# A depthwise convolution moved from VectorE to GpSimd, in pieces of 512 columns, with silu and store one chunk later

## What is computed

```python
def causal_dwconv(x, buf, w):
    width = w.shape[0]
    t = x.shape[1]
    xx = jnp.concatenate([buf.astype(x.dtype), x], axis=1)
    y = xx[:, 0:t, :] * w[0]
    for j in range(1, width):
        y = y + xx[:, j:j + t, :] * w[j]
    return y, xx[:, xx.shape[1] - (width - 1):, :]

c, new_buf = causal_dwconv(qkv, conv_buf, conv_w)
c = jax.nn.silu(c)
```

## Time and profile before

| what | value |
|---|---|
| median of 3 runs | 4591.77 us (4585.16 to 4597.04) |
| the profiled execution | 4549.66 us, its span 4548.4 us |
| PE busy | 3964.1 us, 87% |
| DVE busy | 2130.7 us, 47% |
| ACT busy | 1527.5 us, 34% |
| POOL busy | 689.2 us, 15% |
| mean granted TensorE clock | 0.902 of full speed |

### The profile page before, as it was taken

The page is one execution under the profiler, slowest core; times in us unless marked ns, Lnnn a source line. Parts: engine busy times, 40 slices in busy tenths (PEclk is TensorE's granted clock), DMA queues, the critical chain, the costliest instruction groups (busy, mean ns, idle before and its releaser), DMA issues. The chain is left out here.

```text
span 4548.4 us, 51075 instructions
## 1 busy us (share of the span) xinstructions
PE 3964.1 (87%) x19290; PEld 3133.7 (69%) x19290; DVE 2130.7 (47%) x4240; ACT 1527.5 (34%) x2433; POOL 689.2 (15%) x547
## 2 busy tenths in 40 slices
PE   7789787798769876888888769989999999979999
PEld 4445454455358555777777764479999999958777
DVE  5528988998943683333333332224444444430200
ACT  2115555665645233333333321122222222221211
POOL 0100000000000003222222121111111111124443
PEclk9889898999879687778788789999999999989999
DMA  2242222121142102111111013311212121145433
GB/s 92 78 108 64 59 56 69 35 70 36 45 165 73 36 11 69 30 29 33 29 33 31 25 58 107 102 44 37 56 37 56 37 56 37 47 152 168 130 111 112
DMA packets 286836, 298.41 MB, mean 66 GB/s; under 512 B 33599, under 2 KB 231103, under 8 KB 281626
## 3 DMA queue, kind: packets, MB, share of 16 engines
q1 hardware_dynamic: 271278, 256.80, 19.7%
q0 software_dynamic: 2112, 20.97, 1.2%
q10 hardware_dynamic: 13264, 18.25, 1.2%
HBM read 202.15 MB, written 94.10 MB: 65 GB/s over the span
## 5 line engine op out<-in xcount | busy, mean ns | idle before, releaser
L530 PE MATMUL chan_p_g<-ht,chan_w 128*128 128x412 f32 (+1 forms) x1760 | 678.0, 528 | 62.7 <-ACT chan_flat L578 33.7
L914 PE MATMUL up_p_g<-ht_high,up_wh 128*128 128x412 f32 (+1 forms) x1760 | 617.0, 351 | 0.0
L914 PE MATMUL up_p_g<-ht_low,up_wh 128*128 128x412 f32 (+1 forms) x1760 | 615.0, 349 | 0.0
L914 PE MATMUL up_p_g<-ht_high,up_wl 128*128 128x412 f32 (+1 forms) x1760 | 614.8, 349 | 0.0
L530 PEld LDWEIGHTS chan_p_g<-ht,chan_w 128*128 128x128 f32 x1760 | 341.5, 197 | 310.1 <-issue 230.1
L932 ACT ACTIVATE up_pre<-up_p_g 128x412 f32<-128x412 f32 (+1 forms) x220 | 113.3, 515 | 748.0 <-PE up_p_g L914 748.0
L1294 ACT ACTIVATE chan_signed<-chan_sc,chan_trial 128x512 bf16<-128x512 f32 (+6 forms) x224 | 304.9, 1361 | 148.5 <-DVE chan_trial L1349 127.7
L914 PEld LDWEIGHTS up_p_g<-ht_high,up_wh 128*128 128x128 f32 x1760 | 331.3, 188 | 1.6 <-issue 0.4
L914 PEld LDWEIGHTS up_p_g<-ht_low,up_wh 128*128 128x128 f32 x1760 | 331.2, 188 | 1.2
L914 PEld LDWEIGHTS up_p_g<-ht_high,up_wl 128*128 128x128 f32 x1760 | 331.0, 188 | 0.5
L984 DVE TENSOR_SCALAR up_acc<-up_pre,up_taps 128x2048 f32<-128x2048 f32 x44 | 59.3, 1347 | 573.5 <-ACT up_pre L932 573.5
(11 more groups left out here) (549 smaller groups left out, 6874.9 us busy)
## 6 DMA issues: line engine op xcount, KB each, us to landing
down_a<-scratch_act SPq DMA_DIRECT2D x88, 512.0 KB, 3.7
scratch_act<-up_acc SPq DMA_DIRECT2D x22, 1028.0 KB, 5.2
up_w<-in_w_up SPq DMA_DIRECT2D x44, 512.0 KB, 6.4
chan_iq<-scratch_iq SPq DMA_DIRECT2D x28, 512.0 KB, 7.2
scratch_qkv<-chan_acc SPq DMA_DIRECT2D x12, 1028.0 KB, 4.6
mid_raw<-scratch_qkv SPq DMA_DIRECT2D x16, 768.0 KB, 5.3
chan_w<-in_w_in SPq DMA_DIRECT2D x22, 512.0 KB, 4.6
proj_x<-in_x_prompt SPq DMA_DIRECT2D x16, 512.0 KB, 3.5
```

The source lines that it names most:

```text
L530: last = pe.matmul(p_g[u % BANKS][:, 0:cols.stop - cols.start], weights[:, k, :], K.ht[:, k, cols], start=(k == 0), stop=(k == KD - 1))
L914: last = pe.matmul(p_g[u][:, 0:cols.stop - cols.start], wp[s][:, k, :], hp[:, k, cols], start=(k == 0 and m == 0), stop=(k == KD - 1 and m ...
```

## The change

All four taps go to GpSimd, which does them as soon as the five drains of block v are done. [...] Tap 0 is one TENSOR_SCALAR of 2048 columns. The eight sample columns are TENSOR_SCALARs of their own, added with the last piece. Silu and store move one chunk further on: silu after the second group of chunk v + 2, the store after the third.

```diff
+    PART = SEQ // 4
...
+        tmp = c.sb("tmp", [P, PART + DEC])
...
@@ sync
-                    if idx == 3 and n > IQS and kind(n - 1)[0] == "conv":
-                        v = kind(n - 1)[1]
+                    if idx == 2 and n > IQS + 1 and kind(n - 2)[0] == "conv":
+                        v = kind(n - 2)[1]
                         sp.wait_ge(s_silu, v + 1)
                         sp.dma_start(K.d_qkv[v, :, :], acc[v % 2][:, :]).then_inc(s_st[v % 2], 16)
...
@@ scalar
-                    if idx == 3 and n > IQS and kind(n - 1)[0] == "conv":
-                        v = kind(n - 1)[1]
+                    if idx == 1 and n > IQS + 1 and kind(n - 2)[0] == "conv":
+                        v = kind(n - 2)[1]
                         act.wait_ge(s_conv, v + 1)
...
@@ vector
-            dve.wait_ge(s_taps, 64)
-            for n in range(IQS, CHUNKS):
-                for idx in range(NG):
-                    if idx < 4 and n > IQS and kind(n - 1)[0] == "conv":
-                        if idx == 0:
-                            dve.wait_ge(s_evac, n * NG - FROM)
-                        conv(kind(n - 1)[1], idx)
-                    side.until(share(n * NG + idx, KD))
+            for u in range(FROM, CHUNKS * NG):
+                side.until(share(u, KD))
             side.rest()
+
+        @block.gpsimd
+        def _(pool):
+            step = Chain(pool, s_step)
+            pool.wait_ge(s_taps, 64)
+            pool.wait_ge(s_kept, 1)
+            for n in range(IQS, CHUNKS):
+                what, v = kind(n)
+                if what != "conv":
+                    continue
+                src, out = pre[v % 2], acc[v % 2]
+                old = past[:, v, :].rearrange("p (b j) -> p b j", j=3)
+                tap = lambda i: taps[:, i, v:v + 1]
+                last_of = lambda i: old[:, :, i] if i < 3 else src[:, 3 + SEQ:]
+                if v == 0:
+                    pool.wait_ge(s_mm, FROM)
+                if v:
+                    pool.wait_ge(s_conv, v)
+                if v >= 2:
+                    pool.wait_ge(s_st[v % 2], v // 2 * 16)
+                pool.wait_ge(s_evac, (n + 1) * NG - FROM)
+                pool.tensor_scalar(out[:, 0:SEQ], src[:, 0:SEQ], tap(0), None, ALU.mult)
+                pool.tensor_scalar(out[:, SEQ:], last_of(0), tap(0), None, ALU.mult)
+                for i in range(1, 4):
+                    for at in range(0, SEQ, PART):
+                        final = at + PART == SEQ
+                        if final:
+                            pool.tensor_scalar(tmp[:, PART:], last_of(i), tap(i), None, ALU.mult)
+                        step(pool.tensor_scalar(tmp[:, 0:PART], src[:, at + i:at + PART + i], tap(i), None, ALU.mult))
+                        part = out[:, at:] if final else out[:, at:at + PART]
+                        last = pool.tensor_tensor(part, part, tmp[:, :] if final else tmp[:, 0:PART], ALU.add)
+                        if not final:
+                            step(last)
+                    if i < 3:
+                        step(last)
+                    else:
+                        last.then_inc(s_conv, 1)
```

19 lines of the change are left out of this document (1 added, 18 removed).

## The result

The changed kernel takes 4617.4 us (median of 9 runs, 4601.2 to 4637.2), the kernel before, run beside it, 4585.3 us (9 runs, 4575.1 to 4597.0): a ratio of 1.0068, 95% interval 1.0045 to 1.0091. It is slower, by about 32 us or 0.7%. The forecast was 4743 us and its range began at 4630: the direction was right, the size nearly five times too large.

The account below looks back on a forecast made before the run. In `channels`, TensorE was taken to pace the scores, VectorE search and mask. Searches 120 + scores 60 + masks 30 - 59 saved = +151 us on 4592 gave 4743 us; range 4630 to 4840.

Parts of the forecast that it names:

- VectorE's convolution gone: In `channels`: convolution steps outside the score stretches leave VectorE's path, 59 us saved.
- searches beside GpSimd: Threshold search: a round's two small VectorE operations wait for GpSimd operations, 120 us added.
- scores: Score stretches: VectorE's two-input operations wait for GpSimd until TensorE, without a gap before, must wait; 60 us added.
- masks: Masking of ties: some eleven VectorE operations per pair each wait 0.7 to 1.4 us; 30 us added.
- lateness: GpSimd's 44 us per block is barely in time for ACT in chunk v + 2; nothing added.
- 22 x 2.29 and about six L621: Convolution steps outside score stretches: 22 L624 save 50 us, about six L621 save 9.
- The price of a round: Search: a round beside GpSimd is 1.35 us longer, L1338 waiting 0.7 and L1349 0.65.
- Beside POOL one of them goes between two POOL operations: Scores: one two-input VectorE operation passes between two GpSimd operations, 3.7 us for two units.
- Rival 1: Search: two-column operations aren't held or holds end early; search about 60, +90 us, 4680 us; chance 0.17.
- Rival 2: GpSimd: a TENSOR_SCALAR costs a COPY, 28 us per block; +31 us, 4623 us; chance 0.1.
- Rival 3: GpSimd is late, ACT stands at drain or silu; +60 on top, 4800 us, up to 4850; chance 0.13.
- the two small rivals: Rival 2, and one where exclusion binds long operations alone: -34 us, 4558 us, chance 0.07.

Follow-up runs that it names:

- e2_move_only: The kernel before with only silu and the store moved, the convolution staying on VectorE; ratio to the kernel before 0.9972 (0.9951 to 0.9993).
- e4_no_move: The changed kernel with silu and store put back where the kernel before had them; ratio to the kernel before 1.0242 (1.0206 to 1.0277).
- e2_256: The changed kernel with pieces of 256 columns for all four taps; ratio to the kernel before 1.0158 (1.0104 to 1.0211).
- e1_split0: The changed kernel with tap 0's 2048-column piece cut into four of 512; ratio to the kernel before 1.0008 (0.9986 to 1.0030).

## Why the prediction was wrong in size

| term | forecast | measured |
|---|---|---|
| VectorE's convolution gone | -59 | -73.9 |
| searches beside GpSimd | +120 | +81.1 |
| scores | +60 | +15.4 |
| masks | +30 | +15.3 |
| lateness | 0 | 0 |
| sum | +151 | +37.5 |

The three measured parts make +37.9 us; they leave the last mask out. The difference of two large numbers took on the errors of both, and all four leant the same way.

**Saved.** The principle held: the searches gave 58.9 us for 59.3 us of convolution busy in them, the masks 13.1 for 14.3, the scores 2.2 for 36.8, where TensorE sets the pace. The count failed. "22 x 2.29 and about six L621" came from stretches cut by the clock; cut at the instructions, 24 L624 and 8 L621 lay outside the scores. At the forecast's own prices, 2.29 and 1.5 us, these are 67 us instead of 59, and beside e2_move_only the kernel without convolution gained just that (67.1; 48.6, 13.1 and 5.8 us in the three). The other 6.8 of the 73.9 are the move's, which the forecast had put at nothing.

**Searches.** The price of a round was 1.35 us: L1338 waits 0.7, and L1349 0.65 behind the next operation. Measured, 99 rounds lay beside GpSimd without a long piece and lost 0.60 us on average. In 20 neither of the two was over 0.3 us long, in 54 one (0.56 us lost), in 25 both (1.03). The holds themselves had been read nearly right from one row each: additions to their end, products for two-input operations in their first 0.8 us (0.70 it is); that a product holds L1353 throughout was too much, for seven of 32 found it open or nearly over and nine were let go at 0.71 us. What failed above all is that both waits were charged to every round. They meet an operation by phase, and the loop settles: a product and an addition take 3.0 us together, and a round of 2.2 to 2.7 us can be pulled up to that, seldom beyond (11 of the 99 rounds took 3.1 to 4.0 us). So the larger rounds lose less. The searches of pairs 5 to 7 hold 163 of the 298 us of GpSimd in searches and lost 31 of the 81 us (each against the kernel without convolution). The long piece was right: 3 us forecast, 2.86 on average in ten rounds.

**Scores.** "Beside POOL one of them goes between two POOL operations", 3.7 us for two units. In the stretch from 1139 us on, L1336 in the changed kernel (min/median/max ns):

```profile
L1336 DVE SCALAR_TENSOR_TENSOR chan_sc<-chan_r,chan_iw,chan_sc x14: 737/1175/1780, 1138.1 to 1152.6; 128x512 f32<-128x512 f32 x14
```

From the first start to the fourteenth are 14.5 us, 1.1 a unit, against TensorE's 1.3: with a product and an addition at 1.9 and 1.4 us, three units go by for each pair, not two. It fits under TensorE, whose row for the stretch says so (busy us of TensorE, its weight loads, VectorE, ACT, GpSimd; clock):

```profile
1126.00:1167.00 41.00, 39.84 (x135) 24.22 (x134) 40.83 (x39) 21.65 (x39) 38.80 (x24) 1.00 0.04 12
```

TensorE 97% busy, VectorE now 99.6%: it became almost the bound, and didn't pass it. The kernel with additions only shows the other side: 24.6 us lost in the scores (270.3 - 245.7) instead of 15.4.

**Masks.** Half of the forecast's 30. The price of 0.7 to 1.4 us for each of eleven operations per pair had the same flaw: every one of them was charged a wait. Over the twelve tiles, the largest rise is that of the comparison for equality with the threshold, L1371 before and L1386 after:

```profile
L1371 DVE TENSOR_SCALAR chan_tie<-chan_sc,chan_trial 128x640 bf16<-128x640 f32 (+11 forms) x12 | 10.9, 910 | 0.0
```

```profile
L1386 DVE TENSOR_SCALAR chan_tie<-chan_sc,chan_trial 128x640 bf16<-128x640 f32 (+11 forms) x12 | 16.9, 1405 | 0.0
```

The two SCALAR_TENSOR_TENSORs rose by 0.33 and 0.17 us on average and the scan by 0.11, while the counts and the one-column TENSOR_SCALARs ran as before.

**Right.** GpSimd's 538 us, 45 per block; products at 1.56 us, 1.88 to 1.95 in the scores; the counts untouched; the two small operations longer by 0.29 and 0.21 us on average, nearly the 0.3 to 0.6 named; no silu waiting. The 2048-column product took 5.44 us, not 6.2. Rival 1 had the search at 60 us, nearer to the 81 than the forecast's 120, because a hold ends early; for L1364 behind a product it does. Rival 2's 4623 us, with 60, 15 and 15 us for the three, is near the time and near the terms, but by luck: its reason, a product as cheap as a copy, is not what happened. Rival 3 was not far away: taking the move of silu back brings it (e4_no_move), or 9 us more per block (e2_256). The range began at 4630 because only the two small rivals had scores and masks at less than full price, and both were left outside; the term for the scores had a lower bound of nothing, wherever TensorE stays ahead, and was given none.

## What to carry to other kernels

Work moved to GpSimd is not paid by its busy time but by the moments at which VectorE's two-input and small integer operations meet an operation that holds them: two-input additions hold for their whole length, and long pieces are the dearest; cut them until GpSimd is just in time and no further, because every cut makes GpSimd slower, and being late cost more here than the holds that it saved. Where a loop of VectorE is short, compare its period with the rhythm of GpSimd's chain: most rounds lose no more than the difference, and not the sum of their waits. And where a forecast is the difference of two terms, price each from its own experiment or leave the range open down to the smaller.

## What was not expected of the hardware

A GpSimd product (TENSOR_SCALAR, one tensor input, 512 columns, 1.56 us) held VectorE's two-input operation in its first 0.70 us and no longer, in all 40 cases. The 128x2 TENSOR_SCALAR met two holds in it, one up to 0.71 us and one that caught it from 1.00 us on and lasted to the end, with an open stretch between them. e1_split0, with 44 such meetings, shows the same: released at 0.70 us when it came up to 0.53 us after the start, free from 0.61 to 0.89, held to the end from 0.96 to 1.36. An addition of 512 columns held to its end, and a 2048-column product held the small TENSOR_SCALAR to its end in five cases and the two-input operation to 3.72 us of 5.44 in two. In 256 columns the product held the two-input operation for 0.48 of 0.92 us. What sets these lengths wasn't tried. GpSimd yields as well: beside L1336 its product mostly takes 1.88 to 1.95 us and its addition 1.38 to 1.41, so in the scores both engines lose a little instead of one losing all; beside the long operations of a mask one product of 512 columns took 4.60 us.
